# A gated linear recurrence inside a fused decoder trunk: transposed queries, keys and decays, and column strips for the small levels

## The reference

```python
q = silu(q) * H_DK ** -0.5
forget = lb + (1.0 - lb) * sigmoid(f)
logf = log(maximum(forget, 1e-30))
k = (1.0 - lb) * sigmoid(-f)

def gla_chunk(S, q, k, v, logf):
    G = cumsum(logf, axis=1)
    decay = exp(where(mask, G[:, :, None] - G[:, None, :], MASK_VALUE))
    A = einsum('bnmhd,bmhd->bhnm', q[:, :, None] * decay, k)
    intra = einsum('bhnm,bmhe->bnhe', A, v)
    cross = einsum('bnhd,bhde->bnhe', q * exp(G), S)
    S_new = exp(G[:, -1])[..., None] * S + \
        einsum('bmhd,bmhe->bhde', k * exp(G[:, -1:] - G), v)
    return S_new, intra + cross
o = rmsnorm(o, norm_g)
return silu(g) * o, S
```

## Time and profile before

| | us |
|---|---|
| median of 3 runs | 4242.59 (4240.7 to 4248.35) |
| the profiled execution, its own time | 4243.86 |
| its span | 4242.1 |
| mean granted TensorE clock | 0.926 of 2.4 GHz |

### The profile page before, as it was taken

The page is one execution under the profiler, slowest core; times in us unless marked ns, Lnnn a source line. Parts: engine busy times, 40 slices in busy tenths (PEclk is TensorE's granted clock), DMA queues, the critical chain, the costliest instruction groups (busy, mean ns, idle before and its releaser), DMA issues. The chain is left out here.

```text
span 4242.1 us, 43167 instructions
## 1 busy us (share of the span) xinstructions
PE 3764.1 (89%) x17542; PEld 2619.8 (62%) x17542; DVE 1501.7 (35%) x2591; ACT 754.9 (18%) x1570; POOL 198.6 (5%) x214
## 2 busy tenths in 40 slices
PE   5988899987988789999988889998888787999998
PEld 3544446675656567888845344566666574778887
DVE  2156393145754511000012555912367453110000
ACT  1222222122412100000012222221133121000000
POOL 0000411100000000000000013120000000000000
PEclk9988999798978899999999889998999797999999
DMA  3110443522103021212122124444221211212111
GB/s 122 62 59 33 148 171 122 193 86 75 47 33 100 23 93 60 80 60 75 55 78 82 38 70 157 161 155 142 75 70 45 72 62 52 80 60 80 63 71 56
DMA packets 256368, 357.03 MB, mean 84 GB/s; under 512 B 38206, under 2 KB 144318, under 8 KB 256036
## 3 DMA queue, kind: packets, MB, share of 16 engines
q1 hardware_dynamic: 216060, 254.13, 18.0%
q0 software_dynamic: 21504, 75.51, 5.4%
q10 hardware_dynamic: 18600, 24.55, 1.6%
HBM read 308.27 MB, written 45.89 MB: 83 GB/s over the span
## 5 line engine op out<-in xcount | busy, mean ns | idle before, releaser
L369 PE MATMUL ps<-hT,ring 128*128 128x272 f32 x5632 | 1390.3, 404 | 118.6 <-PEq L156 53.6
L369 PEld LDWEIGHTS ps<-hT,ring 128*128 128x128 f32 x5632 | 1085.0, 196 | 385.2 <-issue 98.3
L361 PE MATMUL ps<-ring,hT 128*128 128x512 f32 (+3 forms) x1728 | 715.8, 556 | 46.5 <-ACT stage L435 24.4
L361 PEld LDWEIGHTS ps<-ring,hT 128*128 128x128 f32 (+1 forms) x1728 | 304.2, 198 | 363.5 <-issue 329.2
L369 PE MATMUL ps<-branchT,ring 128*128 128x272 f32 x1024 | 290.5, 436 | 73.7 <-DVE arena L463 28.6
L2251 PE MATMUL ps<-arena,ring 128*128 128x272 f32 x1408 | 323.7, 393 | 3.0 <-DVE xT L2269 1.9
L2251 PEld LDWEIGHTS ps<-arena,ring 128*128 128x128 f32 x1408 | 267.2, 190 | 59.5 <-issue 2.7
L369 PEld LDWEIGHTS ps<-branchT,ring 128*128 128x128 f32 x1024 | 207.4, 210 | 149.3 <-DVE arena L463 37.9
L477 DVE TENSOR_TENSOR arena<-ps,arena 128x272 f32<-128x272 f32 x88 | 38.9, 442 | 603.7 <-PE ps L369 603.7
L937 DVE MAX8 branchT<-arena 32x8 f32<-32x2080 f32 x64 | 148.2, 2316 | 2.2
L938 DVE MATCH_REPLACE8 arena<-branchT,arena 32x2080 f32<-32x2080 f32 x64 | 146.9, 2296 | 0.0
(11 more groups left out here) (377 smaller groups left out, 3746.6 us busy)
## 6 DMA issues: line engine op xcount, KB each, us to landing
ring<-in_w_in SPq DMA_DIRECT2D x44, 2048.0 KB
ring<-in_w_gu SPq DMA_DIRECT2D x44, 1024.0 KB
spill<-stage ACTq DMA_DIRECT2D x72, 256.0 KB
arena<-spill SPq DMA_DIRECT2D x16, 1024.0 KB, 5.3
ring<-in_w_branch SPq DMA_DIRECT2D x16, 1024.0 KB
ring<-in_w_down SPq DMA_DIRECT2D x8, 2048.0 KB
ring<-in_w_out SPq DMA_DIRECT2D x4, 2048.0 KB
ring<-in_w_down SPq DMA_DIRECT2D x4, 1536.0 KB
```

Of the source, the lines that this page charges most:

```text
L361: mm = pe.matmul(bank[0:m, 0:w], hT[:, c, t0:t0 + m], slot3(j)[:, c, 0:w], start=(c == 0), stop=(c == kn - 1))
L369: mm = pe.matmul(bank[:, 0:HALF], slot3(j)[:, c, at:at + P], src, start=(c == 0), stop=(c == kn - 1))
```

## The change

1. `c0` is projected with channels on partitions, in 8 rows of 8 products of 272 columns, and goes to `spill_q`; `c1` is taken twice by ACT, as sigmoid(f) and sigmoid(-f), and written to two rows of `spill`. The sigmoids and table loads leave `stage_hgrn`.
2. `saved_x` keeps the whole residual (its DMA is twice as long). The queries of all tokens are loaded into its left half, `xT[:, 0:4]`, at the end of the retention stage; `stage_ssm` reads the left half back ahead of its own loads.
3. Level exponents are summed with the channels on partitions: `sf` is the stationary side, and the constants of all levels are the moving side, 8 products of 512 columns a tile. The keys are transposed once (4 transposes). No level needs a transpose.
4. Level scaling works on half the tokens each: 13 tensor_tensor of 128 elements for each pair of heads.
5. The diagonal and the levels 1 to 16 are formed for each block of 32 keys alone: products with 32 stationary and 32 moving columns, 4 to a slot (`mb`), the output in a strip of 32 partitions. Levels 32 and 64 take 4 products a head. In all 28 products a head, 112 a tile.
6. DVE masks the six slots with two instructions and sums them with one reduction; ACT copies the upper blocks (bank 4, cleared once).
7. GpSimd multiplies keys and gate gains; for the sample state it does the 8 decays of 512 elements.
8. The sample rows lie with a head to a strip of 32 partitions: 14 small DMAs load them, 36 output products and 8 state products go to strips, and four banks take the addends.
9. The weights of the share points change from 91 points (sum 174) to 30 points (sum 107), the same 192 steps.

```diff
-            elif name[:2] in ("ga", "wb", "wo", "iq", "xb"):
+            elif name[:2] in ("ga", "wb", "wo", "iq", "xb", "c0"):
...
+                elif name == "c0":
+                    ins = act.activation(st[:, 0:HALF], bank[:, 0:HALF], ACT.Silu)
+                    dst, src = (spill_q[at:at + P, t], st[:, 0:HALF])
...
+                        ins = act.activation(st2[0:m, :], bank[0:m, :], ACT.Sigmoid, scale=-1.0)
+                        dst2, src2 = (spill[4, t0:t0 + m, :], st2[0:m, :])
...
-                    sp.dma_start(saved_x, xT[:, 4:8, :]).then_inc(S("x_saved"), 16)
+                    sp.dma_start(saved_x, xT).then_inc(S("x_saved"), 16)
...
+                    sp.wait_ge(S("x_saved"), 16)
+                    sp.dma_start(xT[:, 0:4, :], spill_q.rearrange("(c p) t -> p c t", p=P)).then_inc(S("q_in"), 16)
...
+            share = Share("wb11", [5] + [3, 3, 4, 4, 4, 3] * 4 + [3, 3, 4, 4, 4])
...
+                        pool.tensor_tensor(k(i), k(i), oml, ALU.mult).then_inc(S("c_k"), 1)
+                        g4 = g(i).rearrange("p (h e) -> p h e", h=4)
+                        pool.tensor_tensor(g4, g4, bc(ghg, 1, 4), ALU.mult).then_inc(S("c_gain"), 1)
...
+                            pool.tensor_tensor(s0, s0, bc(dec[:, half * 4:half * 4 + 4, h], 2, P), ALU.mult).then_inc(S("c_state_decayed"), 1)
...
-                            pe.matmul(ps[zbank[x % 2]][0:m, :], K("lv_sum").rearrange("p (l t) -> p l t", l=7)[0:m, x, 0:m], sf[0:m, :]).then_inc(S("c_lv_z"), 1)
...
+                    def z_sums(i, h):
+                        n = 4 * i + h
+                        for half in range(2):
+                            if h == 0:
+                                pe.wait_ge(S(("c_k_taken", "c_kexp")[half]), i + 1)
+                            else:
+                                pe.wait_ge(S("c_e"), 2 * n - 1 + half)
+                            pe.matmul(ps[(0, 5)[half]][:, :], sf(i)[:, h * P:h * P + P], zsum[:, half * 512:half * 512 + 512]).then_inc(S("c_z"), 1)
+                    def products(i, hp):
+                        pe.wait_ge(S("c_x"), 2 * i + hp + 1)
+                        if hp == 0 and i:
+                            pe.wait_ge(S("c_sp"), i)
+                            pe.wait_ge(S("c_y_taken"), i)
+                        t0 = i * P
+                        for hh in range(2):
+                            h = 2 * hp + hh
+                            x = E[hp][:, hh]
+                            for s in range(6):
+                                bank = ps[1] if s < 4 else ps[2]
+                                at = s % 4 * P + h * NS
+                                for mb in range(4):
+                                    c = slice(mb * 32, mb * 32 + 32)
+                                    left = kT[:, h, c] if s < 2 else x[:, s, c]
+                                    right = qT[:, h, t0 + mb * 32:t0 + mb * 32 + 32] if s == 0 else x[:, s, c]
+                                    pe.matmul(bank[c, at:at + 32], left, right)
+                            for s, mb, n0, n1 in ((6, 0, 32, 64), (6, 2, 96, 128), (7, 0, 64, 128), (7, 1, 64, 128)):
+                                c = slice(mb * 32, mb * 32 + 32)
+                                mm = pe.matmul(ps[4][c, h * P + n0:h * P + n1], x[:, s, c], x[:, s, n0:n1])
...
+                    for i in range(4):
+                        products(i, 0)
+                        share.point("pe", pe)
+                        products(i, 1)
+                        share.point("pe", pe)
+                        if i < 3:
+                            start_tile(i + 1)
+                            z_sums(i + 1, 0)
+                            z_sums(i + 1, 1)
...
+                    for b in range(NB):
+                        for h in range(4):
+                            mm = pe.matmul(ps[3][h * NS:h * NS + NS, 0:P], qm[:, b, h * NS:h * NS + NS], S0[:, b, h, :], start=False, stop=(b == NB - 1))
...
+                            pe.matmul(ps[added[h]][:, :], kds[r], Vx[r, half * 4:half * 4 + 4, :].rearrange("p b e -> p (b e)")).then_inc(S("c_state_add"), 1)
...
+                        for lv in range(7):
+                            w = 1 << lv
+                            xl = halves(x[:, :, 1 + lv, :], w)
+                            dve.tensor_tensor(xl[:, :, :, 1, :], xl[:, :, :, 1, :], halves(q, w)[:, :, :, 1, :], ALU.mult)
+                            if lv:
+                                dve.tensor_tensor(xl[:, :, :, 0, :], xl[:, :, :, 0, :], halves(kT[:, hs, :], w)[:, :, :, 0, :], ALU.mult)
+                        if i and hp == 0:
+                            dve.wait_ge(S("c_out"), i)
+                        dve.tensor_copy(dec2[:, i % 2, hs], x[:, :, 0, P - 1:P].rearrange("p h o -> p (h o)"))
+                        dve.tensor_tensor(QD[:, hs, :], x[:, :, 0, :], q, ALU.mult).then_inc(S("c_x"), 1)
...
+                        dve.tensor_tensor(Dm[:, 0:4], ps[1][:, :].rearrange("p (s h n) -> p s h n", s=4, h=4), bc(mask[:, 0:4], 2, 4), ALU.mult)
+                        L(dve, dve.tensor_tensor(Dm[:, 4:6], ps[2][:, 0:256].rearrange("p (s h n) -> p s h n", s=2, h=4), bc(mask[:, 4:6], 2, 4), ALU.mult))
+                        L(dve, dve.tensor_reduce(R, Dm.rearrange("p s h n -> p h n s"), AX, ALU.add))
+                        dve.wait_ge(S("c_U_taken"), i + 1)
+                        for mb in range(4):
+                            c = slice(mb * 32, mb * 32 + 32)
+                            ins = dve.tensor_copy(A[c, :, c], R[c])
...
+                            dve.wait_ge(S("c_state_decayed"), n + 1)
+                            s0 = S0[:, half * 4:half * 4 + 4, h, :]
+                            dve.tensor_tensor(s0, s0, ps[added[h]][:, :].rearrange("p (b e) -> p b e", b=4), ALU.add).then_inc(S("c_state_new"), 1)
...
+                    for n, row in ((0, 4), (1, 7), (2, 6)):
+                        for h in range(4):
+                            sp.dma_start(s_in[h * NS:h * NS + NS, 0, n * P:n * P + P], spill[row, SEQ:T, h * P:h * P + P]).then_inc(S("c_rows_in"), 16)
...
+                    sp.dma_start(xT[:, 0:4, :], saved_x[:, 0:4, :]).then_inc(S("x_left_back"), 16)
```

More of the change, by code:

```diff
@@ L84, in constants @@
         masks.append((block[:, None] == block[None, :]) & ~right[:, None] & right[None, :])
-        sides.append(right)
     put("lv_sum", np.stack(sums, 1))
-    put("lv_mask", np.stack(masks, 1))
-    put("lv_side", np.stack(sides, 1))
+    put("lv_mask", np.stack([sum(m[:, j * 32:j * 32 + 32] for j in range(4)) for m in masks[:6]], 1))
+    put("lns", np.full((P, 1), np.log(P ** -0.5)))
     lg = np.log1p(-np.exp2(-5.0 - np.arange(4)))
@@ L322, in spilled_by @@
         def spilled_by(name, w):
-            n = sum(1 for row in table[:END[name]] if row[0] not in ("aq", "akv", "iq", "ikiw"))
+            n = sum(2 if row[0] == "c1" else 1 for row in table[:END[name]] if row[0] not in ("aq", "akv", "iq", "ikiw"))
             return 16 * len(range(w, n, 4))
@@ L1492, in stage_hgrn @@
[L1492 to L1500, removed]
-            weights = [4]
-            for i in range(5):
-                weights += [1] * (2 * nlv[i] + 1) + [4, 5, 2, 6, 4]
@@ L1504, in stage_hgrn @@
-            share = Share("wb11", weights)
-            job0 = J["wb11"] - 1
-            zbank = (0, 5)
-            with nc.Block() as block:
+            A = ar.take(4, P)
+            Dm = ar.take(6, 4, NS)
+            kT = ar.take(4, P)
+            sm = ar.take(2, 4)
+            dec2 = ar.take(2, 4)
+            y = Dm.rearrange("p s h n -> p (s h n)")[:, 0:512]
+            st = Arena(stage, 0, 4 * 512)
+            kd = (st.take(512), st.take(512))
+            QD, F2 = st.take(4, P), st.take(512)
@@ new lines, in decays @@
+                    def decays(i, h):
+                        hp = h // 2
+                        if i:
+                            act.wait_ge(S("c_products"), 2 * i + hp - 1)
+                            act.wait_ge(S("c_x"), 2 * i + hp - 1)
+                        for half in range(2):
+                            act.wait_ge(S("c_z"), 2 * (4 * i + h) + half + 1)
+                            act.activation(E[hp][:, h % 2, 4 * half:4 * half + 4].rearrange("p s t -> p (s t)"), ps[(0, 5)[half]][:, :], ACT.Exp).then_inc(S("c_e"), 1)
@@ L1708, in _, with key_decay @@
+                    def key_decay(i):
+                        dve.wait_ge(S("c_kexp"), i + 1)
+                        dve.wait_ge(S("c_k"), i + 1)
+                        dve.tensor_tensor(kd[i % 2], k(i), kd[i % 2], ALU.mult).then_inc(S("c_kd"), 1)
+                    for w in range(4):
+                        dve.wait_ge(S(f"spilled{w}"), spilled_by("dt", w))
+                    L(dve, dve.memset(ps[4][:, :], 0.0))
+                    forget(0)
                     share.point("dve", dve)
-                    forget(0)
@@ L1794, in _ @@
                         for h in range(4):
[L1795 to L1801 removed]
```

(2 more changed lines are left out.)

541 lines of the change are left out of this document (289 added, 252 removed).

## The result

The changed kernel takes 4099.29 us (median of 4 runs, 4094.47 to 4106.7) against 4242.99 for the kernel before on the same chip: ratio 0.9661, 95% interval 0.9644 to 0.9678, 144 us faster. I forecast 85, with a range of 4110 to 4225: the sign was right, the size outside the range.

The account below looks back on a forecast made before the run. PE was taken to bound the kernel, busy 3764 of 4242 us. Terms -31.7 - 61 + 0 + 6 + 2 = -85 against 4243.9 gave 4159, so 4158 for the median; range 4110 to 4225.

Parts of the forecast that it names:

- Term A: Levels of the 8 prompt tiles: small products at 27.5 ns a record save 3.96 us a tile, 31.7 us in all.
- lower bound of 17.5 ns: Prompt-tile small products: record price if the 70 ns overlap four ways, a gain of 50 us in all.
- rival 1: Prompt-tile small products: strips don't overlap at 32 columns, each record costs 70 ns, total 4235 us; chance 0.10.
- bound of +45: Prompt-tile levels: at 70 ns a record, a loss of 5.6 us a tile, 45 in all.
- Term B: Sample tile: 26.7 us of work and waits plus 4 us of clock saved a layer, 61 us in all.
- Terms C and D: Waiting in prompt tiles, taken as 0 with 16 us either way; the stage's start, 3 us slower a layer, +6.
- Rival 2: Prompt tiles: DVE's long scaling holds banks back, PE stands about 4 us more a tile, total 4190; chance 0.20.
- Term E: Work moved between stages (`c0`, `c1`, DMAs, row loads, GpSimd's products): +2 us, bounds 0 and +10.
- Rival 3: Sample tile saves 75 us and PE's idle time in prompt tiles halves, total 4128; with cheaper strips, chance 0.18.
- Rival 4: Prompt tiles: the clock falls to 1.2 GHz during the narrow products, +139 us, total 4306; chance 0.05.
- one of my own signs: Prompt tiles: the prediction is wrong if the clock there falls below 0.9.

Follow-up runs that it names:

- Experiment 5: Changed kernel with the decay projection's two sigmoids and the table loads put back on ScalarE's list in the recurrence stage: 4108.43 us.
- experiment 6: Changed kernel with VectorE emptying the branch rows' banks earlier, after the masks and before and inside a scaling: 4088.41 us.
- experiment 1: Changed kernel with a head pair's small products all sent to one column strip before the next, instead of going round four: 4139.03 us.
- experiment 8: Changed kernel with GpSimd's two 512-element products of each prompt tile (keys and gain) moved to VectorE: 4094.47 us.

## Why the prediction was wrong

**Term A, wrong in size: the price of a small record.** The 16 bursts of the kernel after last 21.8 us together (12 of 1.26, two of 1.33, and 1.97 and 2.06 where the clock was low); 16 times 3.08 were forecast. That is 27 of the missing 59 us. The step that failed is "fewer columns should not cost more", which took the 27.5 ns of a record with 128 moving columns for one with 32. The row gave a price for columns, not for a record: a strip's price is nearly proportional to its columns (116 ns at 128, 30.9 at 32), and a quarter of it or somewhat more is paid when four alternate, down to 11.3 ns. The lower bound of 17.5 ns failed as well, because it divided by four the 70 ns of a row at half clock; so did the price of 70 itself, on which rival 1 and the bound of +45 stand.

The rule of the Trainium skill (TensorEngine Tiling (Array Packing), Instruction Overhead), some 60 cycles for each matmul whatever its columns, is not borne out for a record: 11.3 ns are 27 cycles of 2.4 GHz, and 32 columns are cheaper than 64. For a float32 product of two records, 22.6 ns or 54 cycles, its figure comes close, but its flatness does not hold.

**Term B, right, and a little small.** The sample stretch is 40 us shorter, 41 counted alike (30 to 40 forecast), the clock 0.88 (above 0.85), the wait on the adds 0.8 (below 1). The eight state products took 5.5 us, 4.7 of it work, instead of 7.9, because row strips overlap too; I had only allowed for column strips. That is 3.2 us less work a layer, 6 in both. One reading of mine was wrong without moving the sum: the sample rows were not at full speed until 1231. The granted clock was 0.50 from 1196.11 to 1199.66 and again from 1213.95 to 1218.97, and 1.00 only over the outputs, 1221.87 to 1231.42.

**Terms C and D, wrong: waiting.** PE's idle time in the stage fell by 20.8 us in the first layer and 18.3 in the second. Forecast was 8.4 less at the adds, nothing less in prompt tiles, 3 more at the start, so 5.4. The difference is 15 and 13 us, 28 in all. I had set ACT's shorter list against DVE's longer pieces and called it even. Experiment 5 prices the first at 6.2 us of idle a layer. The second was too high: operations of 128 elements last 0.28 us but start 0.20 apart, so a pair takes 3.0 us instead of 4.2. Rival 2 was real all the same, 8.4 us a layer where 2.8 stood before, and experiment 6 took most of it away. What made the head of a tile fall from 6.4 to 0.3 us, and most of the fall at the gate rows, was not tested apart.

**Term E, wrong in the other direction.** I said that nothing outside would move by more than 3 us. The attention part got 10 us longer over both layers; a table load ahead of an awaited eviction makes 6 of them if the second layer is like the first. I had counted the evictions and not the table, though I had listed loads among what left the stage. The merge part got 3.5 and 3.7 us shorter, but parts outside differ by 0 to 7 us between profiles of runs in which their code is the same (the merge part takes 157.7 to 161.6 us; the part between the two barriers ahead of the first attention part 216.5 us in the changed kernel's profile and 223.7 in that of experiment 1), so the rest is not assigned.

27, 28 and 6 make 61 of the 66 us by which the stage beat its terms (153 against 87); 5 are left, for the sums, totals and transposes of the sample tile, whose removal I had estimated, and for the clock, and were not tested. Rival 1 (strips don't overlap) is refuted by experiment 1. Rival 3 (more waiting goes) was the nearest, 4128, and right in kind on waiting, though it left term A as it was. Rival 4 did not come as I described it: the clock is 1.00 over tile 1 and the bursts there last 1.26 us. But one of my own signs was met: over tile 2 the clock is 0.88, below 0.9. The low stretches stand behind the waits of 3.70 and 3.04 us for DVE's evictions, not at the narrow products, whose two bursts in that tile are at full clock.

## What to carry to other kernels

Before pricing a new small operation by the nearest row, ask what that row's time is made of: columns, records or a change of shape; where there are two rows with different columns, take the slope, and read the granted clock of the stretch in which the row stands. Compare stretches with the same ends: a wait at a barrier that is in one and not in the other looks like a gain. And look at every tile, not at one. Small products that go round four strips, by columns or by rows of the array, run side by side, and are worth it as long as slower work stands between their bursts; look for rows that wait for "issue" when they come faster. When work moves from one stage to another, move its table load in the sum too, and put it where the engine idles, not behind the product that someone waits for; and when an engine gets long unbroken pieces, give it a place inside them to empty banks for others.

## What the runs showed of the hardware

- Float32 records that alternate over four strips cost 11.3 ns each at 32 moving columns, 17 to 19 at 64, 29.4 at 128; in one strip 30.9 at 32 and 116 at 128. All at full clock; at a granted clock of 0.50, in one strip of 32 columns, 53.5.
- Bursts of 224 such records met pauses of 0.3 to 2.4 us with nothing waited for, several of them 256 matmul records apart. Split into bursts of 112 with fill between, they had none; yet one burst of 112 a layer met a pause of 1.1 to 1.3 us in experiment 8, once the wait before it was gone.
- Four products that each use 32 rows of the array, on different rows, overlap: 8 records of 512 columns last 1.14 us together, where 4 took 1.98 before.
- While GpSimd multiplied 512 elements, a DVE copy of 2 elements took 1.24 us instead of 0.16.
- VectorE products of 128 elements last 0.28 to 0.29 us and start 0.20 us apart.
